# Second mixer of a fused three-block kernel: input projection in two halves of the channels, end states and scans of two pieces inside its second half

## The chip, the cores and the metric

The kernel runs on one core of a Trainium2 chip. The metric is the device time of one execution in microseconds (us); lower is better. All data are fp32. Engine names are those of the profile: PE (TensorE matmul), PEld (TensorE weight load), DVE (VectorE), ACT (ScalarE), POOL (GpSimd) and SP (the queue that issues most DMAs). A **pair** is here one weight load and one matmul as the profile records them: each fp32 matmul of the code leaves two pairs, a transpose leaves one.

## The reference, cut to what matters

Three blocks run over 256 tokens of 1024 channels: a gated delta rule mixer with a dense MLP, then an S5 mixer with a mixture of experts, then a pooling and attention block with an MLP. The change touches only the S5 mixer, the "second mixer":

```python
def s5_mixer(x, w_in, lam_re, lam_im, log_dt, b_re, b_im, c_re, c_im, d_skip, w_glu):
    u = (x @ w_in).astype(f32)                       # 256 x 1024 by 1024 x 1024
    a_bar = jnp.exp(lam * dt)
    ...
    def step(h, u_c):
        bu = jnp.einsum('gpc,btgc->btgp', b_bar, u_c.astype(jnp.complex64))
        _, hs = lax.associative_scan(binop, (jnp.broadcast_to(a_bar, bu.shape), bu), axis=1)
        hs = hs + a_pow[None] * h[:, None]
        y = jnp.einsum('gcp,btgp->btgc', c, hs).real
        return hs[:, -1], y
    ...
    y = ... + d_skip.astype(f32) * u
    hid = jax.nn.gelu(y.astype(x.dtype), approximate=False)
    val, gate = jnp.split(hid @ w_glu, 2, axis=-1)
    return val * jax.nn.sigmoid(gate)
```

There are 64 groups of 16 channels with 64 complex states each.

## The kernel before

The state recurrence is cut into sub-chunks of 8 tokens (`SUB`), 32 of them (`NSUB`). Two groups share the 128 partitions as a "pair of groups" `pr`, of which there are 32 (`PAIRS`), handled in four **pieces** of 8. The tables for the powers of the decay are built earlier, beside the first block's MLP, so that the second mixer itself is a fixed order of steps, written out by hand for each engine and tied together with semaphores.

On PE, in program order:

1. **Input projection** (L2175): for each of the 8 residues `s` of a token modulo 8, for each of the 8 channel tiles `k`, four matmuls `q` with 32 stationary columns each (the tokens of that residue, every eighth column of `xT`) against 256 columns of `s5_in_w`. The four go to four column groups of the array. After every second residue `u_done` is raised. 256 matmuls, 512 pairs.
2. **Transposes of u** (L1789, 16 pairs). They wait for the copies of the banks into `u_r`, made half by DVE (L1095, `ur_v`) and half by ACT (L1637, `ur_a`).
3. **End states** (L2198): for each piece, 8 matmuls for the real part and 8 for the imaginary part, 128 stationary columns of `W1T` against 64 columns of `U`; 128 pairs in all. ACT copies each bank into `E` (L1648, `e_read`).
4. **Outputs of a piece** (`y_piece`, L2214 and L2219): 96 pairs each, 16 with 64x32 tiles and 8 with 128x32 tiles in turn, after `h_ready` of that piece. It reads `T[j]`, the skip and kernel blocks, which SP loads from `k_scratch`. Between the pieces stand the transposes of the piece before (4 pairs, after ACT's copy L1656).
5. **GLU product** (L2249), which starts once ACT has made the GELU (L1666) of three pieces, and reads the tiles of the hidden state in the order 0, 4, 1, 5, 2, 6, 3, 7.

DVE works beside it. It first takes the last kernel blocks, then waits for their store to DRAM (`kd_stored`), writes the decay factors of all pieces (L1079 to L1081), builds the rotation table `rot` in five doubling steps (L1086 to L1091), copies its half of u, and then does the four pieces of the **scan**: six operations around `tensor_tensor_scan` (L1108 to L1118), the last of which raises `h_ready`. A scan starts when ACT has copied both end states of its piece. POOL reloads the layer norm's weights into `norm_w` as soon as the norm before is done.

## Time and profile before

| | us |
|---|---|
| median of 3 runs | 1324.07 (1322.55 to 1326.37) |
| the profiled execution | 1323.09 |
| its span | 1321.2 |
| PE busy in the span | 1280.0 (97%) |
| input projection, L2175, in the chain | 28.21 |
| end states, L2198, in the chain | 14.37 |
| from the first projection matmul to the first GLU matmul | 489.52 to 556.18 |

The profiled execution is 1.9 us longer than its span and 1.0 us shorter than the median. The profile is read from the chain of work that ended last. Where a step of it is an engine's work, only less of that work, or faster work, moves the end. Where it is a wait, its releaser counts. A matmul's recorded duration includes its way through the array, so the pace of a row of matmuls is read from their starts, not from their durations.

### The profile page before, as it was taken

How to read it: one execution, taken by the hardware profiler on the slowest of the kernel's cores; microseconds unless marked ns; L12 is line 12 of the kernel's file. 1: busy time of each engine (PE TensorE's matmuls, PEld its weight loads, DVE VectorE, ACT ScalarE, POOL GpSimd, SP SyncE). 2: the span in 40 equal slices, each digit the busy share in tenths (PEclk: the TensorE clock that was granted, in tenths of full speed). 3: DMA queues.
4: the chain of work that ended last, by engine and by line, in shares of the span. 5: the costliest groups of instructions: out<-in, count | busy, mean ns of one | idle time of the engine just before them, and what ended most of it. 6: DMA issues, size and time to landing. Idle time of an engine off the chain costs nothing.

```text
span 1321.2 us, 24403 instructions
## 1 busy us (share of the span) xinstructions
PE 1280.0 (97%) x10751; PEld 902.9 (68%) x10751; DVE 497.1 (38%) x966; ACT 220.6 (17%) x440; POOL 197.9 (15%) x144
## 2 busy tenths in 40 slices
PE   7999999999999999899999999999999979999997
PEld 6888985867677758547566666666646645999443
DVE  0643644253245355523111100111062164565555
ACT  2461341130011111502000010101021021111000
POOL 1026000407566400000200000000034000000000
PEclk9999999999999999999899999999999999999999
DMA  9424010899253188656999999999998150353530
GB/s 344 158 103 155 6 65 0 211 376 301 98 194 101 64 194 103 218 213 239 377 414 416 406 409 421 412 405 407 389 353 233 54 201 0 128 179 143 194 123 32
DMA packets 96934, 292.00 MB, mean 221 GB/s; under 512 B 5917, under 2 KB 43265, under 8 KB 84577
## 3 DMA queue, kind: packets, MB, share of 16 engines
q1 hardware_dynamic: 82288, 260.46, 54.2%
q0 software_dynamic: 4800, 14.67, 3.7%
q10 hardware_dynamic: 9776, 15.86, 3.6%
q8 instruction: 54, 0.88, 0.3%
q14 instruction: 16, 0.12, 0.0%
HBM read 274.19 MB, written 16.78 MB: 220 GB/s over the span
## 4 chain that ended last, share of the span: by engine, by line
PE 93%; DVE 4%; ACT 2%; issue 1%; DMA 0%; POOL 0%; DVEq 0%; ACTq 0%; POOLq 0%
PE bank L1817 19%; PE bank L2314 17%; PE bank L2331 9%; PE bank L2486 8%; PE bank L2524 7%; PE bank L1830 6%; PE bank L2119 5%; PE bank L2249 4%; PE bank L1789 3%; PE bank L2175 2%; PE bank L1823 2%; PE bank L1961 1%; PE bank L2198 1%; PE bank L1947 1%; PE bank L2135 1%
## 5 line engine op out<-in xcount | busy, mean ns | idle before, releaser
L1817 PE MATMUL bank<-xT,arena 128*128 128x256 f32 x1248 | 276.0, 380 | 2.3 <-ACT arena L1521 1.3
L1817 PEld LDWEIGHTS bank<-xT,arena 128*128 128x128 f32 x1248 | 235.5, 190 | 38.2 <-issue 5.3
L2314 PE MATMUL bank<-arena 128*32 128x352 f32 x3072 | 232.1, 464 | 0.7 <-DVE arena L1186 0.7
L2314 PEld LDWEIGHTS bank<-arena 128*32 128x32 f32 x3072 | 129.2, 111 | 100.5 <-issue 6.8
L2331 PE MATMUL bank<-arena 128*32 128x256 f32 x2112 | 115.7, 379 | 0.0
L2331 PEld LDWEIGHTS bank<-arena 128*32 128x32 f32 x2112 | 86.5, 110 | 28.5
L2524 PE MATMUL bank<-arena 128*128 128x512 f32 x224 | 96.7, 593 | 0.7 <-DVE arena L1363 0.7
L1231 DVE TENSOR_TENSOR arena<-arena,bank 128x352 f32<-128x352 f32 x24 | 19.2, 799 | 205.8 <-PE bank L2314 205.8
L2524 PEld LDWEIGHTS bank<-arena 128*128 128x128 f32 x224 | 42.4, 190 | 53.5 <-issue 49.4
L2119 PE MATMUL bank<-arena 128*128 128x512 f32 x144 | 63.6, 595 | 0.0
L1050 DVE TENSOR_TENSOR arena<-arena,bank 128x256 f32<-128x256 f32 x22 | 9.3, 421 | 135.4 <-ACT arena L1612 135.4
L2486 PE MATMUL bank<-arena 128*128 128x128 f32 x512 | 58.5, 275 | 0.0
L2486 PEld LDWEIGHTS bank<-arena 128*128 128x128 f32 x512 | 57.8, 192 | 0.0
L1830 PE MATMUL bank<-arena 128*128 128x512 f32 x128 | 55.9, 593 | 0.5 <-DVE arena L1321 0.5
L1789 PE MATMUL bank<-const,arena 128*128 128x128 f32 x296 | 41.8, 276 | 10.8 <-DVE arena L1331 5.6
L2249 PE MATMUL bank<-arena 128*128 128x512 f32 x112 | 48.5, 593 | 2.6 <-issue 2.6
L2119 PEld LDWEIGHTS bank<-arena 128*128 128x128 f32 x144 | 26.9, 190 | 30.8 <-issue 30.6
L1789 PEld LDWEIGHTS bank<-const,arena 128*128 128x128 f32 x296 | 33.5, 141 | 17.8 <-DVE arena L1331 5.6
L683 POOL TENSOR_TENSOR small<-small 128x1 f32<-128x1 f32 x1 | 0.2, 194 | 302.1 <-DMA slot_rows<-arena 302.1
L2486 PE MATMUL bank<-xT,arena 128*128 128x128 f32 x384 | 44.5, 275 | 0.0
L2486 PEld LDWEIGHTS bank<-xT,arena 128*128 128x128 f32 x384 | 43.8, 192 | 1.0 <-issue 1.0
L1830 PEld LDWEIGHTS bank<-arena 128*128 128x128 f32 x128 | 24.0, 190 | 29.2 <-issue 28.2
(401 smaller groups left out, 1440.7 us busy)
## 6 DMA issues: line engine op xcount, KB each, us to landing
arena<-moe_w SPq DMA_DIRECT2D x64, 1408.0 KB, 14.7
arena<-moe_w SPq DMA_DIRECT2D x24, 1536.0 KB, 16.6
arena<-ffn_w SPq DMA_DIRECT2D x33, 1024.0 KB, 10.3
arena<-gdn_w_in SPq DMA_DIRECT2D x8, 2048.0 KB, 11.4
arena<-w_up SPq DMA_DIRECT2D x8, 2048.0 KB, 8.8
arena<-w_down SPq DMA_DIRECT2D x8, 2048.0 KB, 7.8
slot_rows<-arena ACTq DMA_DIRECT2D x1, 9600.0 KB, 48.2
arena<-s_w_glu SPq DMA_DIRECT2D x4, 2048.0 KB, 11.8
```

The costliest lines, as they stand in the source:

```text
L1231: V_.tensor_tensor(mh[:, t].rearrange("p (x f) -> p f x", x=FE_T), msil[:, t].rearrange("p (f x) -> p f x", x=FE_T), banks[2 * t + 1][:, 0 ...
L1789: return nc.tensor.transpose(dst, src, const[0:k, C_ID, 0:k])
L1817: last = mm(bank[:, at:at + SEQ], w[:, k, P * m:P * m + P], x[:, k, :], start=(k == 0), stop=(k == KT - 1))
L1823: last = mm(bank[:, at + P * n:at + P * n + P], w[:, k, P * m:P * m + P], xT[:, k, P * n:P * n + P], start=(k == 0), stop=(k == KT - 1))
L1830: last = mm(bank, x[:, k0 + k, P * n:P * n + P], w[:, k], start=(k0 + k == 0), stop=(k0 + k == total - 1))
L2119: last = mm(banks[2 * n + hf][:, :], hT[:, c % 2, k, P * n:P * n + P], f2[c % FF_SETS][:, k, 512 * hf:512 * hf + 512], start=(c == 0 and k ...
L2175: last = mm(banks[s // 2][32 * q:32 * q + 32, 256 * (s % 2):256 * (s % 2) + 256], x_sub[:, k, s], w[:, 256 * q:256 * q + 256], start=(k == ...
L2249: last = mm(banks[4 * c + 2 * hf + n][:, :], hidT[:, k, P * n:P * n + P], glu[2 * hf + c][:, k], start=(i == 0), stop=(i == KT - 1))
L2314: last = mm(banks[i][32 * q:32 * q + 32, 0:EW1], xg[:, t, EK * s + kk], w[:, kk, EW1 * q:EW1 * q + EW1], start=(s == 0 and kk == 0), stop= ...
L2331: last = mm(y_bank[t][32 * q:32 * q + 32, 0:EW2], mhT[:, t, 32 * x:32 * x + 32], m2[c][:, x % 3, EW2 * q:EW2 * q + EW2], start=(x == 0), s ...
L2486: last = mm(bank[:, P * m:P * m + P], lhs[:, k, P * m:P * m + P], rhs[:, k], start=(i in (1, 2, 5) and m == k == 0), stop=(k == 3), skip_g ...
L2524: last = mm(d_bank[i][:, :], lhs[:, k], rhs[:, k], start=(d == k == 0), stop=(d == 7 and k == 1))
```

## The change

The projection is cut by channels instead of by pairs of residues. Its first half (`hf` 0) does all 8 residues with the first 128 of each group of 256 weight columns, and the second half does the others. So each matmul has 128 moving columns and there are 512 of them. With the first half done, pieces 0 and 2 have all their inputs. Their transposes, end states and scans are put between parts of the second half, and the pieces are handled in the order 0, 2, 1, 3 from there on.

```diff
+PIECES = (0, 2, 1, 3)
...
-        u_r = region(37376, PAIRS // 2, SUB, GC)
+        u_r = region(40576, PAIRS // 2, SUB, GC)
...
-        decay8 = region(39424, NPIECE, 2, PIECE, NSUB)
-        rot = region(42176, 2, PAIRS, NSUB)
+        decay8 = [region(39424 if j == 3 else 42624 + 512 * j, 2, PIECE, NSUB) for j in range(NPIECE)]
+        rot = flat_w.rearrange("p (a b c) -> p a b c", a=2, b=PAIRS)
...
+        def e_bank(at, ri):
+
+            return banks[(0, 4, 2, 0)[at] + ri]
...
                 pool.wait_ge(norm_done, 4 * n)
+                if n == 2:
+                    pool.wait_ge(h_ready, NPIECE)
                 norm_load(0, "ln_g", n * DM)
```

On DVE the wait for the store of the kernel blocks moves behind the third scan, and the decay factors are written piece by piece:

```diff
-            dve.wait_ge(kd_stored, 16 * NPIECE)
...
+            for j in range(NPIECE - 1):
+                decay_piece(j)
...
-            for j in range(NPIECE):
+            for at, j in enumerate(PIECES):
+                if j == NPIECE - 1:
+                    dve.wait_ge(kd_stored, 16 * NPIECE)
+                    decay_piece(j)
...
-                dve.wait_ge(e_read, 2 * j + 2)
+                dve.wait_ge(e_read, 2 * at + 2)
```

On ACT the copies of u and of the end states alternate. DVE keeps one copy of each kind, and ACT makes three of each:

```diff
+            take_e(0)
+            take_u(0)
+            take_e(1)
+            take_u(1)
+            for i in range(2):
+                act.wait_ge(u_tr, 3 + i)
+                nc.scalar.copy(U[:, 8 + 4 * i:12 + 4 * i].rearrange("p a b c -> p (a b c)"), banks[6 + i][:, :]).then_inc(u_a, 1)
+            take_e(2)
+            take_e(3)
```

On PE:

```diff
+            def s5_input(hf, residues):
+
+                for s in residues:
+                    for k in range(KT):
...
+                        for q in range(4):
+                            last = mm(banks[2 * hf + s // 4][32 * q:32 * q + 32, P * (s % 4):P * (s % 4) + P], x_sub[:, k, s],
+                                      w[:, 256 * q + P * hf:256 * q + P * hf + P], start=(k == 0), stop=(k == KT - 1))
+                    if s % 4 == 3:
+                        last.then_inc(u_done, 1)
...
+            s5_input(0, range(SUB))
+            s5_input(1, (0, 1))
+            pe.wait_ge(ur_v, 1)
+            pe.wait_ge(ur_a, 1)
+            pe.wait_ge(w_in, 16)
+            pe.wait_ge(kd_read, 2 * NPIECE)
+            u_transposes(0)
+            u_transposes(1)
+            s5_input(1, (2, 3))
+            pe.wait_ge(u_v, 1)
+            pe.wait_ge(u_a, 1)
+            end_states(0)
+            s5_input(1, (4, 5, 6, 7))
+            end_states(1)
+            pe.wait_ge(ur_a, 3)
+            u_transposes(2)
+            u_transposes(3)
+            pe.wait_ge(u_a, 3)
+            end_states(2)
+            end_states(3)
...
-                for i, k in enumerate((0, 4, 1, 5, 2, 6, 3, 7)):
+                for i, k in enumerate((0, 4, 2, 6, 1, 5, 3, 7)):
```

PE's order of instructions in the second mixer, from the transposes of the normalised x to the first piece of outputs, before. Names are output and inputs, then partitions x columns of the output, then how many in a row (matmuls of the code, not pairs):

```order
L1789 MATMUL bank<-const,xres 128x128 x8
L2175 MATMUL bank<-arena,xT 32x256 x256
L1789 MATMUL bank<-const,arena 128x128 x16
L2198 MATMUL bank<-arena 128x64 x64
L2214 MATMUL bank<-arena 32x128 x8
L2219 MATMUL bank<-arena 32x128 x4
```

The same place on PE after the change:

```order
L1815 MATMUL bank<-const,xres 128x128 x8
L2203 MATMUL bank<-arena,xT 32x128 x320
L1815 MATMUL bank<-const,arena 128x128 x8
L2203 MATMUL bank<-arena,xT 32x128 x64
L2221 MATMUL bank<-arena 128x64 x16
L2203 MATMUL bank<-arena,xT 32x128 x128
L2221 MATMUL bank<-arena 128x64 x16
L1815 MATMUL bank<-const,arena 128x128 x8
L2221 MATMUL bank<-arena 128x64 x32
L2258 MATMUL bank<-arena 32x128 x8
```

The projection (L2175, now L2203) is in three parts. The transposes of u (L1789, now L1815) are in two, and the end states (L2198, now L2221) in three. The outputs (L2214, now L2258) still come after all of them.

ACT's order at the same place before, from the store of the last kernel blocks to the first copies of outputs:

```order
L1594 DMA k_scratch<-arena 32x8x128
L1637 COPY arena<-bank 128x16x32 x2
L1640 COPY arena<-bank 128x512 x2
L1648 COPY arena<-bank 64x256 x16
L1656 COPY arena<-bank 128x4x8x16 x2
```

And after the change:

```order
L1606 DMA k_scratch<-arena 32x8x128
L1648 COPY arena<-bank 128x8x64
L1650 COPY arena<-bank 128x512
L1659 COPY arena<-bank 64x256 x4
L1665 COPY arena<-bank 128x8x64
L1659 COPY arena<-bank 64x256 x4
L1665 COPY arena<-bank 128x8x64
L1673 COPY arena<-bank 128x512 x2
L1659 COPY arena<-bank 64x256 x8
L1682 COPY arena<-bank 128x4x8x16 x2
```

The copies into `u_r` (L1637, now L1648 and L1665) and those of the transposes (L1640, now L1650 and L1673) now stand on both sides of the copies of the end states (L1648, now L1659).

## Rows read from the trace of the kernel before

**Rows 1.** The page: its span and PE's share.

```profile
span 1321.2 us, 24403 instructions
PE 1280.0 (97%) x10751; PEld 902.9 (68%) x10751; DVE 497.1 (38%) x966; ACT 220.6 (17%) x440; POOL 197.9 (15%) x144
```

**Rows 2.** Chain of work that ended last, 478 to 600: start us, us, what.

```profile
489.52 28.21 PE bank L2175 x512
517.73 0.72 issue
518.46 1.94 PE bank L1789 x16
520.39 14.37 PE bank L2198 x128
534.76 0.57 PE bank L2214 x16
...
535.69 0.57 PE bank L2214 x16
...
553.53 2.65 issue
```

**Rows 3.** Groups by form, 484 to 558: line, engine, names, shapes, count | busy us, mean ns | idle.

```profile
L2175 PE MATMUL bank<-arena,xT 128*32 128x256 f32 x512 | 28.2, 380 | 0.8 <-DVE xT L732 0.8
L2175 PEld LDWEIGHTS bank<-arena,xT 128*32 128x32 f32 x512 | 22.7, 138 | 6.1 <-DVE xT L732 1.0 <-issue 0.2
...
L2098 PE MATMUL bank<-arena 128*32 128x128 f32 x12 | 0.5, 272 | 0.0
```

**Rows 4.** Timeline of PE and PEld at 483, last kernel block: start us, us, what.

```profile
483.16 0.81 PEld L2098 LDWEIGHTS bank<-arena 128*32 128x32 f32 x32 [0.76 <-issue]
483.16 1.08 PE L2098 MATMUL bank<-arena 128*32 128x128 f32 x32
...
484.17 0.70 PE L1794 MATMUL bank<-const 128*128 128x512 f32 x1
```

**Rows 5.** Timeline of DVE and ACT, 500 to 536: start, us, what, idle before.

```profile
502.81 1.30 DVE L1079 COPY arena<-small 128x1024 f32<-128x1024 f32 x2 [10.18 <-DMA k_scratch<-arena]
...
515.46 1.29 DVE L1095 COPY arena<-bank 128x512 f32<-128x512 f32 x2
517.77 0.58 ACT L1637 COPY arena<-bank 128x512 f32<-128x512 f32 x1 [13.55 <-PE bank L2175]
...
519.56 0.59 ACT L1640 COPY arena<-bank 128x512 f32<-128x512 f32 x1 [1.20 <-PE bank L1789]
...
534.80 0.74 ACT L1648 COPY arena<-bank 64x256 f32<-64x256 f32 x2 [1.04 <-PE bank L2198]
```

**Rows 6.** Timeline of PE and PEld at the breaks in their work.

```profile
507.15 0.27 PEld L2175 LDWEIGHTS bank<-arena,xT 128*32 128x32 f32 x8 [0.16 <-issue]
...
534.70 0.64 PE L2214 MATMUL bank<-arena 64*32 64x128 f32 x16
...
541.18 0.62 PE L2214 MATMUL bank<-arena 64*32 64x128 f32 x10
...
542.23 0.42 PE L2214 MATMUL bank<-arena 64*32 64x128 f32 x6 [0.42 <-issue]
...
547.81 0.51 PE L2214 MATMUL bank<-arena 64*32 64x128 f32 x9
...
548.62 0.42 PE L2214 MATMUL bank<-arena 64*32 64x128 f32 x7 [0.30 <-issue]
```

**Rows 7.** The page's DMA queues, the one of instructions: packets, MB, share of 16 engines.

```profile
q8 instruction: 54, 0.88, 0.3%
```

**Rows 8.** DVE's timeline: last operation of the third and of the fourth scan (`h_ready`).

```profile
541.38 0.06 DVE L1118 MEMSET small<- 128x1 f32 x1
...
546.88 0.06 DVE L1118 MEMSET small<- 128x1 f32 x1
```

**Rows 9.** DMA issues by line, 484 to 558: count, KB each, median us to landing.

```profile
arena<-s_w_glu SPq DMA_DIRECT2D x4, 2048.0 KB, 11.8
```

More of the change, by code:

```diff
@@ L394, in by_group @@
         def by_group(bank):
-            return bank[:, :].rearrange("p (s a c) -> p a s c", s=2, c=GC)
+            return bank[:, :].rearrange("p (s a c) -> p a s c", s=4, c=GC)
+        def e_bank(at, ri):
+            return banks[(0, 4, 2, 0)[at] + ri]
         def u_pair(pr):
@@ L1076, in _, with decay_piece @@
             dve.wait_ge(kd_done, 2 * NPIECE)
-            dve.wait_ge(kd_stored, 16 * NPIECE)
-            for part in range(2):
-                V_.tensor_copy(decay8[:, :, part], rho8.rearrange("p (j a) -> p j a", a=PIECE)[:, :, :, None].broadcast_to((P, NPIECE, PIECE, NSUB)))
+            def decay_piece(j):
+                link(V_.tensor_copy(decay8[j], rho8[:, None, PIECE * j:PIECE * j + PIECE, None].broadcast_to((P, 2, PIECE, NSUB))))
+                V_.memset(decay8[j].rearrange("p r a n -> p (r a) n")[:, :, 0:1], 0.0)
+            for j in range(NPIECE - 1):
+                decay_piece(j)
             link(V_.tensor_copy(rot[:, :, :, 0], w8))
-            link(V_.memset(decay8.rearrange("p j r a n -> p (j r a) n")[:, :, 0:1], 0.0))
             for n in (1, 2, 4, 8, 16):
@@ L1634, in _, with take_e, take_u @@
             store_kernel(NPIECE - 1)
-            for i in (1, 3):
-                act.wait_ge(u_done, i + 1)
-                nc.scalar.copy(u_r[:, :, 2 * i:2 * i + 2], by_group(banks[i])).then_inc(ur_a, 1)
-            for j in (1, 3):
-                act.wait_ge(u_tr, j + 1)
-                nc.scalar.copy(U[:, 4 * j:4 * j + 4].rearrange("p a b c -> p (a b c)"), banks[4 + j][:, :]).then_inc(u_a, 1)
-            for j in range(NPIECE):
+            act.wait_ge(u_done, 2)
+            nc.scalar.copy(u_r[:, 0:8, 4:8], by_group(banks[1])).then_inc(ur_a, 1)
+            act.wait_ge(u_tr, 2)
+            nc.scalar.copy(U[:, 4:8].rearrange("p a b c -> p (a b c)"), banks[5][:, :]).then_inc(u_a, 1)
+            def take_e(at):
                 for ri in range(2):
-                    act.wait_ge(e_done, 2 * j + ri + 1)
-                    src = banks[(2 * j + ri) % 4][:, :].rearrange("p (a b c) -> p a b c", a=8, b=2)
+                    act.wait_ge(e_done, 2 * at + ri + 1)
+                    src = e_bank(at, ri)[:, :].rearrange("p (a b c) -> p a b c", a=8, b=2)
                     for gh in range(2):
                         half = slice(64 * gh, 64 * gh + 64)
-                        last = nc.scalar.copy(E[half, ri, 8 * j:8 * j + 8], src[half, :, gh])
+                        last = nc.scalar.copy(E[half, ri, 8 * PIECES[at]:8 * PIECES[at] + 8], src[half, :, gh])
                     last.then_inc(e_read, 1)
+            def take_u(i):
+                act.wait_ge(u_done, 3 + i)
+                nc.scalar.copy(u_r[:, 8:16, 4 * i:4 * i + 4], by_group(banks[2 + i])).then_inc(ur_a, 1)
+            take_e(0)
[7 more added lines that the diff above has]
+            take_e(3)
             def take_y(j):
@@ L2187, in _, with end_states, y_piece @@
                 last.then_inc(u_tr, 1)
-            for j in range(NPIECE):
-                if j < 2:
-                    pe.wait_ge(u_v, j + 1)
-                    pe.wait_ge(u_a, j + 1)
+            def end_states(at):
                 for ri in range(2):
-                    i = 2 * j + ri
-                    if i >= 4:
-                        pe.wait_ge(e_read, i - 3)
+                    if at == 3:
+                        pe.wait_ge(e_read, 2)
                     for a in range(8):
-                        pr = 8 * j + a
-                        last = mm(banks[i % 4][:, 64 * a:64 * a + 64], W1T[:, ri, pr], u_pair(pr), start=True, stop=True)
+                        pr = 8 * PIECES[at] + a
+                        last = mm(e_bank(at, ri)[:, 64 * a:64 * a + 64], W1T[:, ri, pr], u_pair(pr), start=True, stop=True)
                     last.then_inc(e_done, 1)
-            def y_piece(j):
-                pe.wait_ge(h_ready, j + 1)
+            s5_input(0, range(SUB))
[18 more added lines that the diff above has]
+            end_states(3)
+            def y_piece(at):
+                j = PIECES[at]
+                pe.wait_ge(h_ready, at + 1)
                 pe.wait_ge(t_loaded, 32 * SUB * max(j + 1, NPIECE - 1))
-                if j >= 2:
-                    pe.wait_ge(ys_read, j - 1)
+                pe.wait_ge(ys_read, at - 1) if at >= 2 else pe.wait_ge(e_read, 4)
                 for d in range(4):
-                    dst = four(banks[4 + j % 2])[:, d]
+                    dst = four(banks[4 + at % 2])[:, d]
                     for ri in range(2):
```

35 lines of the change are left out of this document (10 added, 25 removed).

## The prediction, made before the changed kernel had run

> **What bounds the kernel now.** PE is busy for 97% of the span [rows 1], so I read the chain of waits through the second mixer first, and asked of every piece of it whether it is PE's own work or a wait [rows 2]. From 489.52 to 534.7 it is almost all work: projection 28.21 us, a wait of 0.72, transposes 1.94, end states 14.37. Then come the outputs, and at the end a wait of 2.65 for the GELUs before the GLU product. The scans are on no piece of this chain. DVE raises the third and fourth `h_ready` at 541.44 and 546.94 [rows 8]. The fourth piece of outputs needs the last one and starts at 547.81 [rows 6], so even the tightest scan is 0.9 us early. Bringing scans forward therefore moves no end by itself. What counts is what happens to PE's own time between 489.52 and the first output matmul at 534.70 [rows 2, 6].
>
> **The pace of the projection.** Before, 512 pairs take 28.21 us, the last matmul lasting 0.38 of it: 27.83 / 511 = 54.5 ns from start to start, or 27.9 us for 512 [rows 2, 3]. The change makes 1024 pairs with half as many columns. No row shows this shape for long, but the kernel blocks have it for a short while: 32 columns of weights, 128 moving columns, four column groups. There 32 pairs take 1.08 us with a last matmul of 0.27, so 0.81 / 31 = 26.1 ns each [rows 3, 4]. Half of the pace before is 27.2 ns. I take 26.7, the middle: 1024 x 26.7 = 27.3 us. That is **-0.6 us** (bounds -1.2 and 0).
>
> **Switches between shapes.** From the last start of those 32 (483.16 + 1.08 - 0.27 = 483.97) to the next matmul with 128 weight columns at 484.17 are 0.20 us, of which 0.03 is the step itself: 0.17 for going from 32 columns to 128 [rows 4]. The way back is in the stretch from the transposes' start at 518.46 to the outputs' start at 534.70, 16.24 us [rows 2, 6]. Its 128 end states take 14.37 and 16 transposes at 109 ns 1.74 (109 ns is 1.94 less the last one's tail, over 16), so about 0.1 is left. The new order has three switches of the first kind and two of the second that the old one lacked: **+0.7 us**.
>
> **The wait that goes.** The transposes started at 518.46, 28.94 us after the projection, which needed 27.9. The 1.0 us of waiting for the copies of u is covered now, since residues 0 and 1 of the second half stand between (128 pairs, 3.4 us, against one ACT copy of 0.58) [rows 2, 5]: **-1.0 us**. The cover holds only if DVE is in time. From 492.63, where it began to wait for the store, it has 12.65 us of factors and rotations (502.81 to 515.46) and a copy of 0.65 to do: ready at about 505.9. PE comes there at 489.52 + 640 x 26.7 ns = 506.6 [rows 5]. The slack is 0.7 us, and any delay of PE adds to it.
>
> **The waits that come.** (a) Transposes 2 and 3 wait for ACT's last copy of u. That copy now stands on ACT's queue behind the end states of piece 2, which PE has only just finished. By the rows at the last end states before: their copies start at 534.80 and take 0.74, then the copy of u 0.58, then 0.11 until PE starts (518.35 to 518.46), so 536.23, where PE would have gone on at 534.6: **+1.6 us** [rows 2, 5]. All that PE has left is queued behind it. (b) End states 2 and 3 then wait for two copies of the transposes, both on ACT, where before DVE shared them. The second group's copy started 1.10 us after the transposes (519.56). ACT is now still at the first one until 0.66 + 0.59 = 1.25. So it ends at 1.84, and PE goes on at 1.95, where 8 transposes alone take 0.87: **+1.1 us** [rows 2, 5].
>
> So far: -0.6 + 0.7 - 1.0 + 1.6 + 1.1 = **+1.8 us**.
>
> **Breaks in PE's supply.** This is the unknown term. Inside a piece of outputs, where nothing is waited for, PE stands still twice: 0.42 us of idle after 541.18 and 0.30 after 547.81, each plus the 0.27 for which the last matmul was still on its way, so 0.7 and 0.55 lost. At 507.15 the weight loads stopped for 0.16 in the middle of the projection, and no matmul was delayed [rows 6]. I counted pairs between these places. From 507.1 to 541.4 there are 190 of the projection, 16, 128, and 178 of outputs, in all 512. From 541.4 to 548.2 there are 128. 128 pairs are 256 instructions, and instructions arrive in packets of 0.88 MB / 54 = 16 KB [rows 7], 64 bytes each if a packet holds 256. So I read them as the borders of packets. Every border interrupts PE's supply, and it shows where PE eats its reserve faster than the break lasts. At 54.5 ns a pair, four borders in the projection cost nothing. At the 38.6 ns of the outputs (24 pairs in 0.93 us [rows 2]), three borders cost 0, 0.7 and 0.55. The new projection has 8 borders (1024 / 128) at 26.7 ns a pair, with less reserve in time than either. Bounds: 0 each, as at the slow pace, and 0.7 each, the worst of the nearer rows, so 0 to 5.6 us. I take the mean of the nearer rows, 0.4: **+3.2 us**.
>
> By the Trainium skill (Runtime: NRT & Kernel Launch, "Instruction fetch mechanics") instructions are refilled in 16 KiB blocks of 256, and crossing a border is mostly hidden. The trace agrees on the size, 16 KB a packet, but not for the outputs, where the gaps lie 128 pairs apart. By that rule this term would be 0; it is the first rival below.
>
> **What costs nothing.** GLU weights are loaded after the last end state, as before; they land in 11.8 us at the median [rows 9], and the GLU product comes 21 us after that state. Both move together. POOL's two loads of the next norm's weights (512 KB each) move from 488 to about 550. They are needed after four GLU products, past 583, and nothing is queued behind them before that. Without that cover they would delay the norm by their landing time. The blocks of piece 3 are loaded after the projection's end, which comes 3 to 5 us nearer to the outputs' start, and they are needed 13.1 us after that start. The last scan: its end states are copied 0.8 after the outputs start, the scan ahead of it ends at about 2.7, then 0.5 of decay factors and 5.5 of scan [rows 8], so 8.7, against 13.1 [rows 6]. Outputs, GELUs and the 2.65 at the end are as before; the order of GLU tiles follows that of the pieces.
>
> **Sum.** +1.8 + 3.2 = +5.0 us on the profiled execution's 1323.09 is 1328.1. That execution is 1.0 below the median of the runs, so for a median 1329.0.
>
> **Rivals.**
>
> *Borders hidden* (not slower). The reserve lasts even at 26.7 ns. For it: four borders in the projection cost nothing. Against it: at 507.15 the loads had already stopped once, at half the pace. It decides if no gap stands inside the new projection. Then +1.8: 1325.9. Chance 0.32.
>
> *Loads or supply set the pace at 128 columns* (much slower). A weight load of the projection, whose columns lie 8 apart, lasts 138 ns; 512 of them fit in 22.7 us of busy time, so at least 3.1 overlap. In the kernel blocks 32 loads of 0.11 lie in 0.81, 4.3 at once [rows 3, 4]. At 27 ns a pair 5.2 would have to. If 4.3 is the most, 32 ns a pair and 32.9 us: +5.6 more. If 3.1, 44 ns and 45.4 us: +18. If the outputs' 38.6 ns is the lasting pace of supply, 39.5 us: +12. So 1331.5 to 1344. Against it: each load keeps its 138 ns as if nothing pressed it, and the outputs' pace holds two switches of shape in every 24 pairs, which explain about 0.3 of the 0.93. Chance 0.13.
>
> The Trainium skill (TensorE: Matmul & The Clock Gate, "Back-to-back issue gap") gives a floor of about 25 ns for a short matmul, and 81 ns for a sustained load and matmul of 128 columns. By the latter the projection would take an estimated 83 us, 55 more than now. The 26 ns of the kernel blocks speak against it [rows 4].
>
> *The breaks in the outputs are waits for scans after all* (0.07, with all other ways down). They lie 0 to 1.3 us after `h_ready` [rows 6, 8]. Earlier scans would then take away 1.25: +0.6 without borders in the projection. Even this is not faster by more than a measurement shows.
>
> **Chances.** About 0.3% (4.0 us) can be told from no change. Likeliest case: 0.48, spread over 0 to 5.6 for the borders. A good part of it, from about +4.0 up, is slower; the rest is within. With the rivals: slower 0.52, within 0.3% 0.42, faster 0.06. The range goes from 1323.5 (below the hidden case by the runs' own spread) to 1335.0, which takes in the worst borders (+7.4) and the low end of the loads' rival. Beyond it lie the 38.6 ns and 44 ns cases.
>
> **What would show each step.** The projection's rows: 1024 matmuls whose starts sum to 27 to 28 us without gaps. Gaps of 0.2 to 0.9 us, "issue", 128 pairs apart, inside it: the borders. A wait of PE of about 1.6 us ahead of the later transposes, released by ACT's copy of u, and one of about 1.1 ahead of the third end states. No wait for `h_ready` anywhere. First output matmul 1.8 us (no borders) to 5 us later than 534.7. The prediction is wrong if projection starts step by over 30 ns, or if the stretch from the outputs' start to the GLU product changes from its 21.5 us by over 1 us.

## The result, and the profile of the changed kernel

The changed kernel takes 1337.26 us (median of 4 runs, 1333.67 to 1339.74); the kernel before takes 1324.03 beside it (1322.55 to 1326.37). The ratio is 1.0085, with a 95% interval of 1.0063 to 1.0108; the plain medians lie 13.2 us apart. The prediction said 1329.0, and at most 1335.0. The direction was right and the size was not: +13.2 instead of +5.0.

The page of the changed kernel: its span and its engines, and the granted clock of PE in 40 slices (9 is full).

```profile
span 1337.6 us, 25431 instructions
...
PE 1293.1 (97%) x11263; PEld 994.9 (74%) x11263; DVE 496.5 (37%) x969; ACT 221.9 (17%) x442; POOL 198.1 (15%) x144
...
PEclk9999999999999999799799999999999999999999
```

The span is 16.4 us longer than that in [rows 1]; the profiled execution (1339.74) is the longest of the four. PE is "busy" for 97% in both, so busy time does not tell what happened. The clock line does. It has a 7 in the slice that begins at 535 us. The kernel before has 9 there; its only dent is an 8 in the slice where the router of the mixture of experts runs, behind this mixer; it is the second 7 here.

The chain of work that ended last, from the projection to the GLU product (start us, us, what), as in [rows 2]:

```profile
491.99 5.69 PE bank L2203 x198
497.68 1.29 issue
498.97 3.73 PE bank L2203 x128
502.70 0.82 issue
503.52 9.42 PE bank L2203 x314
...
517.63 3.71 PE bank L2221 x32
521.34 7.15 PE bank L2203 x256
528.50 3.73 PE bank L2221 x32
...
533.02 0.59 ACT arena L1665
533.66 1.98 PE bank L1815 x8
535.66 0.59 ACT arena L1673
536.30 13.92 PE bank L2221 x64
550.22 1.01 PE bank L2258 x16
...
564.57 0.46 issue
...
569.94 2.65 issue
572.60 27.70 PE bank L2291 x64
```

L2203 is now the projection, L1815 the transposes, L2221 the end states, L2258 the outputs, L2291 the GLU product. The first end states take 3.71 and 3.73 us for 32 pairs. The last take 13.92 for 64: 217 ns each, where those before took 112. Nothing is waited for inside that row. Weight loads, matmuls and shapes are those of the row at 528.50. The table by stretches of time shows what differs (us, busy time of each engine with its instructions, PE's granted clock, DMA share, GB/s):

```profile
525.00:530.00 5.00, 5.00 (x143) 4.83 (x135) 2.59 (x7) 0.00 (x0) 0.00 (x0) 1.00 0.08 19
530.00:535.00 5.00, 3.56 (x27) 3.42 (x27) 1.94 (x4) 2.25 (x6) 0.00 (x0) 0.83 0.51 107
535.00:540.00 5.00, 4.33 (x21) 3.92 (x20) 3.42 (x8) 0.98 (x2) 0.00 (x0) 0.50 0.92 90
540.00:545.00 5.00, 5.00 (x25) 5.00 (x25) 0.80 (x2) 1.47 (x4) 0.00 (x0) 0.50 0.00 0
...
550.00:555.00 5.00, 5.00 (x90) 2.64 (x89) 4.07 (x8) 0.73 (x2) 0.00 (x0) 0.63 0.68 221
```

PE's clock is granted in full (2.4 GHz) until 533.25 us and at half (1.2 GHz) from there to 553.75; 25 pairs then start in 5 us; at the pace of [rows 2], 128 in 14.37 us, it would be 45. The second piece's end states start at 528.43 and are through with their steps of 112 ns at 532.03. From there to the transposes at 533.66 PE stands in the new wait (a), 1.63 us, and the fall comes in it, 1.2 us after its start. The prediction counted this wait and nothing behind it.

**What the half clock costs here.** The last 64 end states take 13.85 us from start to start (536.30 to the first output matmul at 550.15). With the full clock the same code takes 7.29 (experiment 1 below). That is 6.56. Transposes and wait (b) take 2.64 instead of 2.10: 0.54. The first three steps of the outputs take 4.28 (550.15 to 554.43) instead of 2.78: 1.50. In all **8.6 us**. First projection matmul to first GLU matmul is 66.66 us before and 80.61 now, 13.95 more. Without the clock it would be 5.35 more, where the sum of the prediction had 5.0.

The rest of the 16.4 lies ahead: the projection starts 2.47 us later (491.99, not 489.52), in code that is the same. In these two profiles nearly all of it is lost in the first matmuls of the first block, the kernel before above:

```profile
12.99 14.05 PE L1817 MATMUL bank<-xT,arena 128*128 128x256 f32 x64 [0.96 <-ACT xT L1473]
...
13.12 16.39 PE L1843 MATMUL bank<-xT,arena 128*128 128x256 f32 x64 [0.85 <-ACT xT L1485]
```

The granted clock is recorded as 1.00 there in both. The projection's start wandered between 489.2 and 492.8 in the profiles of all kernels, the one before with an added wait among them.

The same stretch in all profiles (us; "broken" is first projection matmul to first transpose, less 640 pairs at 27.3 ns and one switch of 0.17, for those that have the new order; "half clock" counts only up to the GLU product):

| kernel | projection to outputs | outputs to GLU | broken | half clock | median | ratio |
|---|---|---|---|---|---|---|
| before | 45.18 | 21.48 | | 0 | 1324.0 | |
| after | 58.16 | 22.45 | 3.24 | 20.5 | 1337.3 | 1.0085 |
| after, again | 56.11 | 22.08 | 1.59 | 20.5 | 1339.0 | 1.0119 |
| 1 `e1_u_first` | 50.13 | 21.60 | 3.93 | 0 | 1329.8 | 1.0043 |
| 2 `e2_filled` | 53.57 | 21.84 | 5.07 | 0 | 1335.7 | 1.0060 |
| 3 `e3_wait_in_before` | 51.46 | 22.18 | | 14.0 | 1331.0 | 1.0051 |
| 4 `e7_wait_in_projection` | 46.60 | 21.48 | | 0 | 1327.6 | 1.0018 |
| 5 `e4_halves_only` | 64.17 | 22.61 | | 31.0 | 1345.4 | 1.0144 |
| 6 `e5_covered` | 49.27 | 21.62 | 4.39 | 0 | 1328.4 | 1.0036 |
| 7 `e6_tables_late` | 55.16 | 22.53 | 0.20 | 20.75 | 1335.7 | 1.0093 |
| 8 `e9_covered_tables_late` | 45.31 | 21.49 | 0.0 | 0 | 1327.8 | 1.0022 |

Ratios are each against the kernel before on the same chip, whose medians were 1324.49 for rows 1 to 4, 1323.30 for 5 to 7 and "again", 1324.04 for 8.

The table leaves out the falls behind this stretch. One stands at the start of the GLU product, about 3.5 us long in the profiles of experiments 1, 2, 4, 7 and of the changed kernel run again, and 7 us in that of 5. In experiment 4 (as above):

```profile
559.00:564.00 5.00, 4.43 (x7) 1.92 (x8) 0.00 (x0) 4.33 (x6) 0.00 (x0) 0.66 1.05 399
```

It stands behind the wait of 2.65 us for the GELUs, which the kernel before, the first profile of the changed kernel and experiments 3, 6 and 8 have without a fall. So one and the same wait is followed by a fall in some executions and not in others. Such a fall costs about 1.7 us: from the first GLU matmul to the end of the span are 765.0 us before, 766.8 in experiment 1 and 766.7 in experiment 4.

### The profile page after: what moved, and what is told of

Same layout as the page of the kernel before. It is cut to its first block, busy times and chain, and to the rows that moved or that the text cites. A ratio compares the mean times of both kernels' runs of the same rounds, so it can differ in the third digit from the quotient of the medians.

```text
span 1337.6 us, 25431 instructions
## 1 busy us (share of the span) xinstructions
PE 1293.1 (97%) x11263; PEld 994.9 (74%) x11263; DVE 496.5 (37%) x969; ACT 221.9 (17%) x442; POOL 198.1 (15%) x144
## 4 chain that ended last, share of the span: by engine, by line
PE 92%; DVE 4%; ACT 2%; issue 1%; DMA 0%; POOL 0%; DVEq 0%; ACTq 0%; POOLq 0%
PE bank L1843 19%; PE bank L2356 17%; PE bank L2373 9%; PE bank L2528 7%; PE bank L2566 7%; PE bank L1856 6%; PE bank L2145 5%; PE bank L2291 4%; PE bank L1815 3%; PE bank L2203 2%; PE bank L1849 2%; PE bank L2221 2%; PE bank L1987 1%; PE bank L1973 1%; PE bank L2161 1%
## 5 line engine op out<-in xcount | busy, mean ns | idle before, releaser
L2356 PEld LDWEIGHTS bank<-arena 128*32 128x32 f32 x3072 | 196.3, 111 | 33.8 <-issue 6.6
L2373 PEld LDWEIGHTS bank<-arena 128*32 128x32 f32 x2112 | 97.6, 110 | 17.3
L1815 PE MATMUL bank<-const,arena 128*128 128x128 f32 x296 | 42.9, 280 | 11.6 <-DVE arena L1343 5.6
L2291 PE MATMUL bank<-arena 128*128 128x512 f32 x112 | 48.5, 593 | 2.7 <-issue 2.7
L1815 PEld LDWEIGHTS bank<-const,arena 128*128 128x128 f32 x296 | 34.2, 143 | 18.4 <-DVE arena L1343 5.6
## 6 DMA issues: line engine op xcount, KB each, us to landing
arena<-moe_w SPq DMA_DIRECT2D x64, 1408.0 KB, 14.4
```

Source lines behind the costliest of these rows:

```text
L1815: return nc.tensor.transpose(dst, src, const[0:k, C_ID, 0:k])
L2291: last = mm(banks[4 * c + 2 * hf + n][:, :], hidT[:, k, P * n:P * n + P], glu[2 * hf + c][:, k], start=(i == 0), stop=(i == KT - 1))
L2356: last = mm(banks[i][32 * q:32 * q + 32, 0:EW1], xg[:, t, EK * s + kk], w[:, kk, EW1 * q:EW1 * q + EW1], start=(s == 0 and kk == 0), stop= ...
L2373: last = mm(y_bank[t][32 * q:32 * q + 32, 0:EW2], mhT[:, t, 32 * x:32 * x + 32], m2[c][:, x % 3, EW2 * q:EW2 * q + EW2], start=(x == 0), s ...
```

## Experiments

The theory after the result: **the wait among the end states makes PE's clock fall, and the fall costs more than the wait**. The rivals: the end states are slow for another reason of the new order (banks, `W1T` beside the table loads), so that they stay slow when the wait is gone; or any wait of this length in this stretch lowers the clock; or the breaks in the projection, not the wait, prepare the fall.

### 1. The wait taken away: ACT copies u first

ACT takes both banks of u before the end states of the second piece, so PE doesn't wait before transposes 2 and 3. Wait (b) stays.

```diff
             take_e(0)
             take_u(0)
-            take_e(1)
             take_u(1)
+            take_e(1)
```

> The changed kernel, but ACT copies both banks of u of the second half before the end states of piece 2, so PE no longer waits ahead of transposes 2 and 3. Theory A (the idle 1.4 us there, right behind end states, made PE's granted clock fall to half from 533.2 to 553.8 us): the clock stays at 1.00 in this stretch, and with the wait (1.6 us) some 8.9 us of half-clock work go: about 1326.8. Theory B (the clock falls in this stretch because of the work itself, the mixed order of projection, transposes and end states with its breaks): the clock still falls, only the wait goes: about 1335.7.

1329.75 us (10 runs, 1326.35 to 1334.29), 1.0043 (1.0027 to 1.0060). PE's timeline (start us, us, what, idle before):

```profile
530.44 1.05 PE L1815 MATMUL bank<-const,arena 128*128 128x128 f32 x8
532.54 7.36 PE L2221 MATMUL bank<-arena 128*128 128x64 f32 x64 [1.05 <-ACT arena L1673]
```

The 64 end states take 7.36 us, and the clock is 1.00 in all of 525 to 545. The slowness goes with the wait, in the same order of work, the same banks and with the same table loads. A wait of 1.05 (b) is still there, and the clock does not fall behind it. The breaks are there too, larger than before (3.93 us), so they don't prepare the fall by themselves. The stretch is 5.07 us longer than before, and the terms say 3.93 of breaks + 1.23 of wait (b) - 1.0 for u + 0.7 for switches = 4.9.

The time is 3 us above the 1326.8 of theory A. The profile accounts for 0.7 by larger breaks and 1.7 by the fall at the GLU product. The runs are not all alike either: the three longest (1332.33 to 1334.29) have a mean clock of 0.986 to 0.989, where the kernel before beside them has 0.990 to 0.995 and experiment 6, in which wait (b) is gone too, 0.992 to 0.994. So in some executions the clock falls once more, perhaps behind wait (b); no trace of such a run exists.

### 2. The wait filled

Three matmuls of constants into a free bank (6 pairs) stand in the place of wait (a).

```diff
             end_states(1)
+            keep_warm(banks[6], 3)
             pe.wait_ge(ur_a, 3)
```

> The changed kernel, with 3 idle-filling matmuls (512 columns, 1.3 us at full clock, results unused) put on PE ahead of its wait for the copy of u; the wait itself stays. Theory A: the clock stays at 1.00 until the outputs, time falls by about 8.9 us to 1328.4. Theory B: no change, 1337.3, the clock falls as before.

1335.68 us (7 runs, 1329.22 to 1339.06), 1.0060 (1.0034 to 1.0085). PE's timeline, and two stretches as above:

```profile
534.66 2.79 PE L1820 MATMUL bank<-const 128*128 128x512 f32 x6
537.29 1.04 PE L1815 MATMUL bank<-const,arena 128*128 128x128 f32 x8
539.06 7.36 PE L2221 MATMUL bank<-arena 128*128 128x64 f32 x64 [0.73 <-ACT arena L1673]
```

```profile
535.00:540.00 5.00, 4.27 (x22) 2.64 (x21) 4.25 (x7) 2.26 (x5) 0.00 (x0) 1.00 0.77 132
540.00:545.00 5.00, 5.00 (x47) 5.00 (x47) 2.41 (x8) 1.80 (x5) 0.00 (x0) 1.00 0.34 30
```

In the trace the theory holds. The wait for the same copy is filled with work, and the clock stays, the 64 end states take 7.36. In the time it missed: 8.9 us less was expected, and the median is 1.6 less than the changed kernel's. The trace accounts for a part. The filling lasts 2.63 where the wait lasted 1.63, and the projection was broken for 5.07 us instead of 3.24. 80.61 - 8.6 + 1.0 + 1.8 = 74.8, and 75.4 was measured for the stretch. Against the execution of before, this one is 15.1 us longer: 8.7 in the stretch, 3.3 in the projection's start, and 3.1 behind the stretch. The trace has more half clock in both of these parts: about 7 us from 29 on, in the first block, and about 3.5 each at the start of the GLU product and at 1101, where 56 matmuls take 26.00 us and 24.30 before. Of the first:

```profile
30.00:36.00 6.00, 6.00 (x18) 5.03 (x18) 1.80 (x9) 4.00 (x7) 0.00 (x0) 0.50 1.04 383
```

But the clock does not explain all runs. They spread over 10 us with mean clocks of 0.987 to 0.994, and the longest (1339.06) has 0.992. What this kernel shows is the clock behind the filled wait, not the price.

### 3. The wait alone, in the kernel before

ACT makes one more copy of 0.6 us behind its copies of the second piece's end states, and PE waits for it in its loop of end states. All else is as before.

```diff
+                if j == 1:
+                    nc.scalar.copy(region(0, 512), banks[6][:, :]).then_inc(ur_a, 1)
...
+                if j == 2:
+                    pe.wait_ge(ur_a, 3)
```

> The kernel before, with one wait added: PE waits between the end states of pieces 1 and 2 for one more ACT copy (its result is not used) that stands behind ACT's copies of the end states; PE is idle for about 1.5 us as in the changed kernel. Nothing else of the change is in it. Theory A: the clock falls to 0.50 after this wait for some 20 us; +1.5 of wait and about +9 of slow work: 1334.5. Theory B: +1.5 only, 1325.6, clock 1.00.

1331.04 us (8 runs, 1329.20 to 1333.63), 1.0051 (1.0036 to 1.0065): 6.6 us. PE's timeline and two stretches:

```profile
521.89 7.33 PE L2202 MATMUL bank<-arena 128*128 128x64 f32 x64
530.66 12.31 PE L2202 MATMUL bank<-arena 128*128 128x64 f32 x64 [1.44 <-ACT arena L1651]
```

```profile
530.00:535.00 5.00, 4.34 (x28) 4.34 (x29) 4.83 (x11) 1.32 (x3) 0.00 (x0) 0.74 0.01 1
535.00:540.00 5.00, 5.00 (x26) 5.00 (x25) 4.80 (x12) 1.13 (x4) 0.00 (x0) 0.50 0.00 0
```

This is the plainest of the runs. 64 end states ahead of the wait take 7.33, and 64 behind it take 12.31. A wait of 1.44 us costs 6.3 up to the outputs, 1.6 of it for itself, and 0.7 more up to the GLU product. The half clock held from 532.25 to 546.25; here it began 1.6 us after the wait had ended, in the changed kernel 0.4 us before. All eight runs have a mean clock of 0.986 to 0.990. It is less than expected, 14.0 us at half and not 20, and 6.6 us in time and not 10. Nothing of the halves, of the new order of pieces or of the table loads is in this kernel.

### 4. The same wait inside the projection of before

ACT makes two copies ahead of that of bank 3, and PE waits for them in the projection, after residue 5 of 0 to 7. PE's later waits for `u_a` count two more.

```diff
+                if i == 3:
+                    act.wait_ge(u_done, 3)
+                    for r in range(2):
+                        nc.scalar.copy(region(10240 + 512 * r, 512), banks[1][:, :]).then_inc(u_a, 1)
...
+                if s == 5:
+                    pe.wait_ge(u_a, 2)
```

> The kernel before, with a wait of PE of about 1.6 us put inside the projection, after residue 5 (two ACT copies, results not used). It is as long as the one in e3, but has projection work on both sides. Theory A (what stands ahead of the idle time counts too; the changed kernel's two breaks of 1.3 and 0.8 us inside the projection left the clock at 1.00): clock 1.00, +1.6, 1325.7. Theory C (any idle of this length brings the clock down): clock 0.50 behind it, +10 or more, 1334 to 1336.

1327.62 us (10 runs, 1325.44 to 1329.57), 1.0018 (1.0005 to 1.0032). PE's timeline and the stretch behind the wait:

```profile
513.96 7.14 PE L2179 MATMUL bank<-arena,xT 128*32 128x256 f32 x128 [1.17 <-ACT arena L1639]
```

```profile
515.00:520.00 5.00, 5.00 (x100) 3.75 (x96) 2.34 (x4) 0.00 (x0) 0.00 (x0) 1.00 0.02 5
```

The wait costs about itself, 1.42 in the stretch, and the clock stays at 1.00 up to the GLU product. The rest of the 3.1 us between the medians is not this stretch: the profile has the fall at the GLU product (1.7) and a start of the projection at 491.49. So the second rival falls: not every wait of this size in this stretch does it. The breaks of 1.29 to 2.02 us in the new projection say the same. What PE does around the idle time seems to count. Inside the projection, with 54.5 (or 27.3) ns a pair in four column groups, no profile has a fall behind idle time; next to the end states, whose matmuls have 64 columns, or the transposes ahead of them, a wait of over 1.4 us was followed by one in all five profiles that have such a wait (both of the changed kernel, experiments 3, 5 and 7), and one of 1.05 us (experiment 1) was not. The idle time here was 0.27 shorter than in experiment 3, but that of the breaks, up to 2.02, was longer, and the clock stayed too.

### 5. The halves alone

All 1024 pairs, then all transposes, then all end states; the order 0, 2, 1, 3 stays. Nothing is mixed in any more.

```diff
             s5_input(0, range(SUB))
-            s5_input(1, (0, 1))
+            s5_input(1, range(SUB))
...
             u_transposes(0)
             u_transposes(1)
-            s5_input(1, (2, 3))
...
             pe.wait_ge(ur_a, 3)
             u_transposes(2)
             u_transposes(3)
-            pe.wait_ge(u_a, 3)
-            end_states(2)
-            end_states(3)
+            pe.wait_ge(u_v, 1)
+            pe.wait_ge(u_a, 3)
+            for at in range(NPIECE):
+                end_states(at)
```

> Projection by halves of the channels and the new piece order, but nothing is mixed into it: all 1024 pairs, then all transposes, then all end states. It measures the pace of the narrow matmuls and the breaks at the instruction borders by themselves. Theory A (pace about 27 ns; breaks of up to 2 us every 128 pairs while DMAs are busy; the clock stays at 1.00 because nothing waits among the end states): projection 27.2 plus 3 to 5 us of breaks, a wait of about 0.7 at the transposes, 4 us longer than before in all: about 1328. A rival that gives the projection's mixed order the blame for the breaks: projection 27 to 28 us without gaps, about 1324.

1345.41 us (10 runs), 1.0144 (1.0109 to 1.0180). Eight runs lie between 1343.4 and 1348.0, two at 1329.5 and 1329.8. PE's timeline in the profiled one:

```profile
524.71 1.09 PE L1813 MATMUL bank<-const,arena 128*128 128x128 f32 x8 [1.65 <-ACT arena L1665]
526.62 26.93 PE L2219 MATMUL bank<-arena 128*128 128x64 f32 x128 [0.82 <-ACT arena L1671]
```

My expectation, 1328 with a full clock, missed by 17 us, and it is the most telling miss. I had made two waits of my own around eight transposes, 1.65 and 0.82 us, and now all 128 end states run at half clock: 26.93 us instead of 14.4. The half clock lasts 31.0 us. The mean clocks of the runs go with their times: 0.991 and 0.993 in the two short ones, 0.978 to 0.982 in the others. So the fall is not certain behind such waits; by these clocks it came in 8 runs of 10.

What the experiment was made for came out as expected. From the projection's start (489.32) to the first transposes (521.97) are 32.65 us; less 1024 pairs at 27.3 ns and one switch, 4.5 us are breaks, where 3 to 5 were expected. So mixing the work is not what causes them.

### 6. Both waits covered

As experiment 1, and the end states of the second piece are cut in two: the real half before transposes 2 and 3, the imaginary half behind them. ACT's part stands first, then PE's.

```diff
             take_u(0)
-            take_e(1)
             take_u(1)
+            take_e(1, (0,))
...
+            take_e(1, (1,))
...
-            end_states(1)
+            end_states(1, (0,))
             pe.wait_ge(ur_a, 3)
             u_transposes(2)
             u_transposes(3)
+            end_states(1, (1,))
```

> The changed kernel with both new waits covered: ACT copies u of the second half first, and PE puts the transposes between the real and the imaginary end states of piece 2. Theory A: neither the 1.4 nor the 1.05 us of idle time is left, the clock stays at 1.00 there; 1 us below the kernel with only the first wait gone, 1328 to 1329. Theory B (the waits only matter as waits): 2.7 us below the changed kernel, 1334.6. If mixing itself brings something, it must fall below 1324.

1328.37 us (7 runs, 1326.29 to 1332.04), 1.0036 (1.0024 to 1.0049), as expected. No wait and no fall are left in the stretch, only the breaks. PE's timeline:

```profile
499.04 3.73 PE L2204 MATMUL bank<-arena,xT 128*32 128x128 f32 x128 [1.85 <-issue]
504.13 3.73 PE L2204 MATMUL bank<-arena,xT 128*32 128x128 f32 x128 [1.37 <-issue]
...
531.80 9.04 PE L2222 MATMUL bank<-arena 128*128 128x64 f32 x80
```

The gaps stand after pair 198 and 128 pairs later, as the prediction had said for the borders. They are larger than it allowed: 1.85 + 0.27 lost at one border, where its upper bound was 0.7. The stretch is 4.23 longer than before: 4.39 of breaks - 1.0 + 0.7 = 4.1. Against the changed kernel on the same chip (1339.04), the two rearranged waits are worth 10.7 us, of which 2.9 are the waits themselves.

### 7. The table loads of pieces 1 and 2 later

SP holds the 32 loads of pieces 1 and 2 from `k_scratch` back until the first half of the projection is done.

```diff
             for j in range(NPIECE - 1):
+                if j:
+                    sp.wait_ge(u_done, 2)
                 table_loads(j)
```

> The changed kernel, but SP holds back the table loads of pieces 1 and 2 until the first half of the projection is done (u_done 2), so few DMAs run until about 505 us and many run after it. Theory D (a break at an instruction border is a fetch that comes late behind other DMAs): the breaks at pairs 198 and 326 shrink below 0.5 us, and breaks of 0.5 us or more show at later borders, past 505 us. Rival E (the breaks belong to these places of the program): they stay at 198 and 326 with 1.3 and 0.8 us. Time within 2 us of the changed kernel in either case, since the waits stay and so the fall of the clock.

1335.70 us (4 runs, 1334.49 to 1337.47), 1.0093 (1.0076 to 1.0110). PE's timeline, and the stretches of the projection (PE's clock, DMA share and GB/s are the last three):

```profile
489.43 17.91 PE L2205 MATMUL bank<-arena,xT 128*32 128x128 f32 x640 [0.78 <-DVE xT L741]
...
520.70 3.06 PE L2205 MATMUL bank<-arena,xT 128*32 128x128 f32 x100 [0.45 <-issue]
```

```profile
490.00:500.00 10.00, 10.00 (x376) 10.00 (x372) 9.12 (x39) 0.00 (x0) 0.00 (x0) 1.00 0.09 21
...
510.00:520.00 10.00, 10.00 (x264) 9.76 (x257) 3.35 (x6) 2.06 (x5) 0.00 (x0) 1.00 0.79 108
```

With the DMA engines 9% busy, 640 pairs run without one gap, 27.6 ns each. The one gap that is left stands at pair 924, where the loads now run; gaps of 0.5 us or more were expected there, and it has 0.45. In the changed kernel the DMA share was 1.01 from 495 to 505, and both gaps lie there. So a border can cost something when other DMAs fill the engines at that time. It doesn't have to: counted on by 128 pairs, the two borders ahead of pair 924 lie at about 510 and 516.5 us, the second where the share is 1.01 (515 to 520), and neither shows a gap. Nor do the three in the projection of before that lie ahead of 510 us, at 54.5 ns a pair and a share of 1.15 to 1.26. The fall of the clock is untouched by this (20.75 us at half, and the last 64 end states again take 13.92). The two causes are independent.

### 8. Both waits covered and the tables late

Experiments 6 and 7 in one kernel.

> The changed kernel with both new waits covered and the table loads of two pieces held back until the first half of the projection is done. Theory A with D: neither the clock's fall nor the breaks; first projection matmul to first output matmul in 45.5 to 46.5 us, against 45.2 in the kernel before, and a time of 1324 to 1325.5, no different from before. If mixing the work gains anything by itself it must show here: below 1322.

1327.76 us (10 runs, 1322.55 to 1329.64), 1.0022 (1.0007 to 1.0037). PE's timeline:

```profile
491.63 17.70 PE L2206 MATMUL bank<-arena,xT 128*32 128x128 f32 x640 [0.78 <-DVE xT L741]
...
517.66 7.66 PE L2206 MATMUL bank<-arena,xT 128*32 128x128 f32 x256
...
527.97 9.04 PE L2224 MATMUL bank<-arena 128*128 128x64 f32 x80
536.94 0.64 PE L2262 MATMUL bank<-arena 64*32 64x128 f32 x16
```

There is nothing left to repair in this stretch. The first part takes 45.31 us, 45.5 to 46.5 were expected, and both together 45.31 + 21.49 = 66.80 against 66.66 before. That is the worth of the mixing itself: nothing. The scans are earlier, and that brings no end forward. The median is still 3.7 us above that of before, and 2 above what was expected. The profiled execution (1325.34) is 2.3 above that of before, and 2.1 of it is the projection's start (491.63, not 489.52), ahead of all that was changed. Why the median is higher stays open.

### 9 and 10. Filling the thin spot of the router

Both kernels have the other fall of the clock, in the router. In the kernel before (stretches as above):

```profile
625.00:630.00 5.00, 5.00 (x18) 3.97 (x18) 2.73 (x17) 0.50 (x2) 0.00 (x0) 0.50 1.01 407
```

It runs from 622.75 to 640.0, behind matmuls of 8 and 96 columns, and no wait of over 0.3 us stands within 4 us ahead of it. I filled this spot with matmuls of constants in the kernel before, and put five more ahead of the GLU product.

```diff
+            keep_warm(banks[0], 5)
             pe.wait_ge(hid_ready, 12)
...
             gather(0, 0)
+            keep_warm(banks[0], 2)
             need_x()
             token_major(banks[2][:, 0:8], xT, w_router, 1).then_inc(route_done, 1)
+            keep_warm(banks[0], 2)
             gather(1, 0)
```

> The kernel before with filling matmuls only: 5 of 512 columns in the 2.65 us wait ahead of the GLU product, and 4 more between the narrow matmuls of the router, where the trace of before shows the clock at 0.50 from 622.8 to 640. Results of the filling are not used. If thin work on PE is what lets the clock fall there as well, the four cost 1.7 us and the 17 us at half clock shrink, which is worth up to 8 us: 1317 to 1322. If not, +1.7: 1325.

1327.17 us (10 runs, 1325.41 to 1329.63) beside 1324.04, 1.0016 (1.0004 to 1.0028). The same stretch of time:

```profile
625.00:630.00 5.00, 5.00 (x28) 3.93 (x26) 1.76 (x11) 0.49 (x2) 0.00 (x0) 1.00 1.02 410
```

The half clock in the router shrinks from 17 us to 3.5, and the kernel becomes 3.1 us slower, where 2 to 7 less were expected. PE's timeline at the first expert, of the kernel before and then of this one:

```profile
633.92 11.54 PE L2314 MATMUL bank<-arena 128*32 128x352 f32 x109 [0.73 <-DVE arena L1186]
```

```profile
636.56 8.65 PE L2317 MATMUL bank<-arena 128*32 128x352 f32 x83 [0.73 <-DVE arena L1186]
```

The profiled execution is 4.3 us longer than that of before, and the router has only a part in it. From the first output to the GLU product are 2.0 more, 1.5 of them for the filling ahead of the product. From the first GLU matmul to the first expert are 77.74 us before and 78.67 now, so the filling in the router costs 0.9 more than the clock gives back up to there; only 0.1 comes back in the experts. And 1.7 is another half clock of 3.5 us at 1090, which the profile of before does not have. So the 3.1 us is not the price of the filling in the router alone.

With experiment 8 added (`e10_all`) it is the same:

> The kernel of e9 with the filling matmuls of e8 as well. The sum of the two: e9's time plus e8's difference to the kernel before, 1318 to 1326.

1327.38 us (10 runs, 1325.86 to 1330.24), 1.0023 (1.0009 to 1.0036), above the 1318 to 1326 that were expected. No version was faster than the kernel before.

### The changed kernel once more

> The changed kernel once more, beside the others on one chip: 1337 within 2 us, with the clock at 0.50 for 14 to 21 us behind the wait for the copy of u.

1339.04 us (4 runs, 1338.00 to 1340.31), 1.0119 (1.0102 to 1.0136). Half clock for 20.5 us again, and 64 end states in 13.92 again. Its breaks were smaller, 1.59 us.

## Why the prediction was wrong

**The step that failed** is "Outputs, GELUs and the 2.65 at the end are as before", and with it the end states, whose 14.37 us were taken over from [rows 2] as they stood. The sum treated PE's pace as a property of the instruction. It counted what PE loses in the new waits while it stands still, and never asked what they do to the work behind them. The missing term is 8.6 us, more than the whole of the rest. The profile of before had a hint. The clock line of its page has an 8, and 17 us of the router ran at half clock; I had not read that line, and no rival was about it. Experiments 1 and 3 show the cause from both sides: with the wait taken away the fall is gone from the stretch, and the wait alone, put into the kernel before, costs 6.6 us.

The test written into the prediction, that the stretch from the outputs' start to the GLU product changes by over 1 us, came out at 0.97 (21.48 to 22.45). It was just not met, since a break less in the outputs (one of 0.46 us, where [rows 6] has two) hid part of the 1.50.

**The other terms**, from the first projection matmul to the first output matmul:

| term | forecast | measured | from |
|---|---|---|---|
| pace of the narrow pairs | -0.6 | 0.0 | 128 pairs: (3.73 - 0.27) / 127 = 27.2 ns; e9: (17.70 - 0.27) / 639 = 27.3 |
| switches of shape | +0.7 | +0.7 | experiment 8: 45.31, less 27.95 + 0.44 + 1.74 + 14.37 of work and a break, is 0.8; 0.1 of it was there before |
| wait for u gone | -1.0 | -1.0 | no idle time before 512.87 |
| wait (a) | +1.6 | +1.63 | 532.03 to 533.66 |
| wait (b) | +1.1 | +1.23 | 530.44 to 532.54 in experiment 1, less 0.87 |
| borders | +3.2 | +3.24 | 512.87 - 491.99, less 17.47 and 0.17 (the second profile: 1.59) |
| PE's clock | none | +7.1 | 6.56 + 0.54 (1.50 more behind it) |
| sum | +5.0 | +12.9 | 58.16 - 45.18 = 12.98 |

*Pace.* At exactly half of the 54.5 ns of before there is no gain in narrower matmuls. The 26.1 ns of the kernel blocks [rows 4], 32 pairs long, was not the lasting value. The middle between two rows was the wrong choice; the row of the same work was right.

*Waits.* Both are as worked out from the rows, in place, releaser and length. PE's timeline of the changed kernel at (a):

```profile
533.66 1.97 PE L1815 MATMUL bank<-const,arena 128*128 128x128 f32 x8 [1.45 <-ACT arena L1665]
```


*Borders.* The sum is right and its making is not. Two borders were open, not eight: 1.29 + 0.27 and 0.82 + 0.27, and some 0.6 is spread over the 314 pairs behind them. In other executions the same place lost 1.6 to 5.1. Each can cost up to 2.3 us, and not 0.7, or nothing, as with the DMA engines 9% busy (experiments 7 and 8). The mean of two near rows times eight met it by luck. The Trainium skill (Runtime: NRT & Kernel Launch, "Instruction fetch mechanics") has such a crossing mostly hidden. The trace disagrees at the two borders where PE takes a pair every 27 ns and table loads run beside it, and agrees where they don't.

*The rivals.* Hidden borders (+1.8) fell with these gaps. The weight loads as a limit fell with 27.3 ns a pair over 640 pairs without a gap: 138 ns of strided weight load for each pair are hidden, 138 / 27.3 = 5.1 at once on the mean, where the rival had 4.3 as the most. The 81 ns that the Trainium skill gives for a sustained load and matmul of 128 columns (TensorE: Matmul & The Clock Gate, "Back-to-back issue gap") does not hold for four column groups in turn. Waits for scans fell too: PE waits for `h_ready` nowhere in the changed kernel, as before; the break of 0.46 in its outputs has no releaser.

**What was right**: scans brought forward move no end (experiment 8: 66.80 against 66.66), the direction, and every cost but one.

**What stays open.** Why a wait of 1.4 us lowers the clock at one place and not at another, and the 2.65 us ahead of the GLU product in one execution and not in another. The runs show that a wait next to the end states is what brings the fall in this stretch; that the work around it decides is likely, from few places, and how it does is not shown. Also the 3.7 us by which experiment 8's median lies over that of before, and the long runs of experiment 2 at a high mean clock.

## What to carry to other kernels

When a change puts a wait into PE's work, price it twice: what it idles, and what the work behind it costs at half clock; read the granted clock line and the stretches at less than 1.00 before forecasting, as they show where a kernel is already thin. A wait of 1.5 us among narrow matmuls can cost 6 to 10 us with the work behind it, and moving one copy of 0.6 us on the engine that releases it took 7.5 us back (experiment 1). Where PE already has no gaps and no scan or transfer is late, as here, mixing pieces of work is worth nothing, and twice as many pairs of half the length brought more instruction borders and no gain in pace.

## What the hardware showed that I had not expected

- A wait of 1.44 us between end states (64 columns, 112 ns a pair) was followed by 14.0 us of half clock; waits of 1.63 in the changed kernel by 20.5; of 1.65 and 0.82 in experiment 5 by 31.0, and in two of its ten runs by no such stretch, by their mean clocks. Idle time of 1.2 to 2.0 us inside the projection was followed by none, and 2.65 ahead of the GLU product by 3.5 to 7 us in six profiles and by none in five others without filling there. By the Trainium skill (TensorE: Matmul & The Clock Gate, "HAM oscillation — how this bites in real kernels") PE goes back to the lower clock when, in a loop, each piece of work is shorter than the wait behind it. The trace shows the return without such a loop: one wait of 1.44 us behind 9 us of unbroken work was enough, and PE then worked on at half clock for 14 us.
- While it is at half clock, PE counts as busy: 97% in both kernels, 13 us apart.
- The clock fell in the router without any wait of over 0.3 us close ahead (622.75 in the kernel before). Filling kept it up for all but 3.5 us of the 17, and up to the first expert it cost 0.9 us more than it brought.
- What I read as an instruction border cost nothing with the DMA engines 9% busy, and up to 2.3 us (experiment 2) at the same pace with the table loads beside it.
